# Even attention of a two-layer backbone: values and probabilities split into high and low fp32r parts

## The reference, cut to what matters

```python
att = block_attention(q, concat([k_ctx, k]), concat([v_ctx, v]), scale)   # latent queries
att_ctx = block_attention(q_ctx, k_ctx, v_ctx, scale)                     # context queries

def block_attention(q, k, v, scale):       # swept over blocks of 128 queries
    s = einsum('bqgrd,bkgd->bgrqk', q_blk, k) * scale
    p = softmax(s, axis=-1)
    return einsum('bgrqk,bkgd->bqgrd', p, v)
```

## Time and profile before

| | us |
|---|---|
| median of 3 runs (1912.35 to 1914.12) | 1913.68 |
| the profiled execution's own time | 1911.99 |
| its span | 1910.1 |
| even attention in the trace | 236.6 to 382 |
| TensorE, VectorE, ScalarE, GpSimd busy over the span | 1792.2, 1141.0, 678.4, 178.9 |

### The profile page before, as it was taken

The page is one execution under the profiler, slowest core; times in us unless marked ns, Lnnn a source line. Parts: engine busy times, 40 slices in busy tenths (PEclk is TensorE's granted clock), DMA queues, the critical chain, the costliest instruction groups (busy, mean ns, idle before and its releaser), DMA issues.

```text
span 1910.1 us, 24356 instructions
## 1 busy us (share of the span) xinstructions
PE 1792.2 (94%) x9558; PEld 1503.3 (79%) x9558; DVE 1141.0 (60%) x1750; ACT 678.4 (36%) x1114; POOL 178.9 (9%) x197
## 2 busy tenths in 40 slices
PE   5999889899999999999999999789978899999998
PEld 3677789777888888887777889669966688888776
DVE  3566667667756666644353778877753644434544
ACT  3333156534522222222343431144443442323342
POOL 1168400000300000000000200111100010000000
PEclk9999989999999999999999999899998999999999
DMA  8333100032133345422121121100002222222221
GB/s 327 123 136 111 45 1 1 2 114 85 78 130 133 125 165 187 167 98 81 52 83 50 54 104 67 44 23 1 1 1 98 78 68 108 88 103 94 96 103 66
DMA packets 30996, 166.80 MB, mean 87 GB/s; under 512 B 4144, under 2 KB 4656, under 8 KB 16688
## 3 DMA queue, kind: packets, MB, share of 16 engines
q1 hardware_dynamic: 29024, 163.60, 23.7%
q10 hardware_dynamic: 1872, 1.82, 0.3%
HBM read 163.31 MB, written 2.10 MB: 87 GB/s over the span
## 4 chain that ended last, share of the span: by engine, by line
PE 83%; DVE 6%; issue 4%; ACT 3%; DMA 1%; DVEq 1%; POOL 1%; POOLq 0%; ACTq 0%; SPq 0%
PE PS L302 12%; PE PS L306 12%; PE PS L304 11%; PE PS L603 7%; PE PS L605 7%; PE PS L604 7%; PE PS L1074 5%; PE PS L344 2%; PE PS L345 2%; PE PS L346 2%; PE PS L1062 2%; DVE w_lo L291 1%; PE PS L336 1%; PE PS L337 1%; PE PS L335 1%
## 5 line engine op out<-in xcount | busy, mean ns | idle before, releaser
L302 PE MATMUL PS<-HT,w_hi 128*128 128x512 f32 (+1 forms) x1232 | 376.7, 354 | 11.5 <-DVE HT L517 6.1
L306 PE MATMUL PS<-HT,w_lo 128*128 128x512 f32 (+1 forms) x1232 | 370.0, 349 | 0.0
L304 PE MATMUL PS<-HT,w_hi 128*128 128x512 f32 (+1 forms) x1232 | 369.2, 348 | 0.0
L291 DVE TENSOR_TENSOR w_lo<-w_raw,w_hi 128x2048 fp32r<-128x2048 f32 x103 | 236.7, 2299 | 162.1 <-ACT w_hi L285 156.2
L603 PE MATMUL PS<-w_hi,a_ring 128*128 128x512 f32 x680 | 275.2, 405 | 15.0 <-DVE a_ring L676 8.0
L604 PE MATMUL PS<-w_lo,a_ring 128*128 128x512 f32 x680 | 267.2, 393 | 0.0
L285 ACT ACTIVATE w_hi<-w_raw 128x2048 fp32r<-128x2048 f32 x103 | 196.3, 1906 | 153.9 <-PEq L635 69.6
L302 PEld LDWEIGHTS PS<-HT,w_hi 128*128 128x128 f32 x1232 | 206.1, 189 | 53.7 <-DVE HT L517 6.6
L306 PEld LDWEIGHTS PS<-HT,w_lo 128*128 128x128 f32 x1232 | 205.9, 189 | 30.8
L304 PEld LDWEIGHTS PS<-HT,w_hi 128*128 128x128 f32 x1232 | 205.9, 189 | 30.7
L973 DVE SCALAR_TENSOR_TENSOR yb<-PS,cws,yb 128x511 f32<-128x511 f32 (+1 forms) x132 | 83.2, 658 | 168.9 <-ACTq L939 165.0
(11 more groups left out here) (307 smaller groups left out, 2845.6 us busy)
## 6 DMA issues: line engine op xcount, KB each, us to landing
w_raw<-wpack SPq DMA_DIRECT2D x103, 1024.0 KB, 4.8
m_raw<-modu SPq DMA_DIRECT2D x80, 512.0 KB, 4.0
mod_raw<-modw SPq DMA_DIRECT2D x8, 1024.0 KB, 11.7
X<-x SPq DMA_DIRECT2D x1, 2048.0 KB, 9.0
out<-X SPq DMA_DIRECT2D x4, 512.0 KB, 2.6
X<-ctx SPq DMA_DIRECT2D x1, 1024.0 KB, 11.3
alnb<-aln ACTq DMA_DIRECT2D x1, 512.0 KB, 4.2
csn<-rope_ev ACTq DMA_DIRECT2D x1, 256.0 KB, 2.5
```

The costliest lines, as they stand in the source:

```text
L291: nc.vector.tensor_tensor(w_lo[r][:, :], w_raw[r][:, :], w_hi[r][:, :].bitcast(F32), ALU.subtract).then_inc(wl_ready, 1)
L302: nc.tensor.matmul(o, wh, xh, start=start, stop=False)
L304: nc.tensor.matmul(o, wh, xl, start=False, stop=False)
L306: last = nc.tensor.matmul(o, wl, xh, start=False, stop=stop)
```

## The change

The even attention gets four functions of its own; the odd attention keeps the old ones.

- Values are kept as `Vh` (rounded by ScalarE) and `Vl` (the difference, by VectorE, once). The transposed probabilities are copied from PSUM to `PTh` by ScalarE as before, rounded now, and VectorE takes the difference of PSUM and `PTh` to `PTl`.
- The value product is three fp32r products per key tile: `Vh` by `PTh`, `Vl` by `PTh`, `Vh` by `PTl`. For the latent units it is made once for two units (256 columns), after the transposes of the next even unit; for the context units once per unit (128 columns).
- TensorE's transposes of u wait until the low part of u-1 has been taken from banks 4 and 5.
- VectorE takes only the reciprocal, into `rinv`; GpSimd multiplies the probabilities by it.
- VectorE copies the output once for two latent units, and in context unit u it copies that of u-1, at the end of the iteration.
- `mod_products` waits for both slots of a pair on one semaphore.

```diff
+        rinv = const("rinv", [P, 2])
...
-        Vev = at("Vev", R_HT + 6 * KIB, [P, NT, 256])
-        PTe = [at(f"PTe{i}", R_HT + (12 + 3 * i) * KIB, [P, TOK]) for i in range(2)]
+        Vh = at("Vh", R_HT + 6 * KIB, [P, NT, 256], F32R)
+        Vl = at("Vl", R_A + 60 * KIB, [P, NT, 256], F32R)
+        PTh = [at(f"PTh{i}", off, [P, NT, 2, P], F32R) for i, off in enumerate((R_HT + 12 * KIB, R_HT + 40 * KIB))]
+        PTl = [at(f"PTl{i}", off, [P, NT, 2, P], F32R) for i, off in enumerate((R_MOD, R_GM))]
...
-        mod_landed = [sem(f"mod_landed{i}") for i in range(KD)]
+        mod_landed = [sem(f"mod_landed{i}") for i in range(4)]
...
+            pe.wait_ge(mod_landed[c], 32)
             for i in range(2):
-                pe.wait_ge(mod_landed[2 * c + i], 16)
...
+        PAIRED = HEADS * LT
+        def products_done(u):
+            return u // 2 + 1 if u < PAIRED else PAIRED // 2 + u - PAIRED + 1
+        def turned_into(u):
+            return (u // 2 % 2, u % 2) if u < PAIRED else (u % 2, 0)
+        def even_pe(pe):
+            U = units(False)
...
+            def scores(u):
+                h, t, nk, k0 = U[u]
+                pe.wait_ge(S("eva", "qTl"), u + 1)
+                if u >= 2:
+                    pe.wait_ge(S("eva", "exp"), u - 1)
...
+                last.then_inc(S("eva", "s"), 1)
+            def values(u, w):
+                h, t, nk, k0 = U[u]
+                b, i = turned_into(u)
+                pe.wait_ge(S("eva", "pTl"), u + w)
+                if products_done(u) > 1:
+                    pe.wait_ge(S("eva", "ocopy"), products_done(u) - 1)
+                else:
+                    pe.wait_ge(S("eva", "vl"), 1)
+                o = PS[:, 7, 0:w * P]
+                for j in range(nk):
+                    vh, vl = (v[:, k0 + j, h // 4 * P:h // 4 * P + P] for v in (Vh, Vl))
+                    ph, pl = (p[:, j, i:i + w, :] for p in (PTh[b], PTl[b]))
+                    nc.tensor.matmul(o, vh, ph, start=j == 0, stop=False)
+                    nc.tensor.matmul(o, vl, ph, start=False, stop=False)
+                    last = nc.tensor.matmul(o, vh, pl, start=False, stop=j == nk - 1)
+                last.then_inc(S("eva", "o"), 1)
+            for u in range(2):
+                q_transpose(u)
+                scores(u)
+            q_transpose(2)
+            for u, (h, t, nk, k0) in enumerate(U):
+                pe.wait_ge(S("eva", "p"), u + 1)
+                if u >= 1:
+                    pe.wait_ge(S("eva", "pTl"), u)
+                for j in range(nk):
+                    last = nc.tensor.transpose(ps2(4, TOK)[:, j * P:(j + 1) * P], Pe[u % 3][:, j * P:(j + 1) * P], ident[:, :])
+                last.then_inc(S("eva", "ptr"), 1)
+                if u % 2 == 0 and 2 <= u <= PAIRED:
+                    values(u - 2, 2)
+                if u > PAIRED:
+                    values(u - 1, 1)
+                if u + 2 < len(U):
+                    scores(u + 2)
+                if u + 3 < len(U):
+                    q_transpose(u + 3)
+            values(len(U) - 1, 1)
+        def even_act(act, scale):
+            U = units(False)
...
+            def exps(u):
+                n = U[u][2] * P
+                if u >= 3:
+                    act.wait_ge(S("eva", "ptr"), u - 2)
+                act.wait_ge(S("eva", "max"), u + 1)
+                nc.scalar.activation(Pe[u % 3][:, 0:n], ps2(2 * (u % 2), n), ACT.Exp, bias=rmax[:, u % 2:u % 2 + 1],
+                                     scale=scale, accum_out=rsum[:, u % 2:u % 2 + 1]).then_inc(S("eva", "exp"), 1)
+            for u in range(3):
+                q_copy(u)
+            exps(0)
+            for u, (h, t, nk, k0) in enumerate(U):
+                if u + 1 < len(U):
+                    exps(u + 1)
+                act.wait_ge(S("eva", "ptr"), u + 1)
+                b, i = turned_into(u)
+                if u >= 4:
+                    reader = u // 2 * 2 - 4 if u < PAIRED else (PAIRED - 4 + 2 * (u - PAIRED) if u < PAIRED + 2 else u - 2)
+                    act.wait_ge(S("eva", "o"), products_done(reader))
+                nc.scalar.activation(PTh[b][:, 0:nk, i, :], ps2(4, nk * P).rearrange("p (j q) -> p j q", q=P), ACT.Copy)\
+                    .then_inc(S("eva", "pT"), 1)
+                if u + 3 < len(U):
+                    q_copy(u + 3)
+        def even_dve(dve, scale):
+            U = units(False)
+            def maxima(u):
+                dve.wait_ge(S("eva", "s"), u + 1)
+                if u >= 2:
+                    dve.wait_ge(S("eva", "exp"), u - 1)
+                m = rmax[:, u % 2:u % 2 + 1]
+                nc.vector.reduce_max(m, ps2(2 * (u % 2), U[u][2] * P), AX_X)
+                dve.drain()
+                nc.vector.tensor_scalar(m, m, -scale, None, ALU.mult).then_inc(S("eva", "max"), 1)
+            def inverse(u):
+                dve.wait_ge(S("eva", "exp"), u + 1)
+                if u >= 2:
+                    dve.wait_ge(S("eva", "p"), u - 1)
+                nc.vector.reciprocal(rinv[:, u % 2:u % 2 + 1], rsum[:, u % 2:u % 2 + 1]).then_inc(S("eva", "inv"), 1)
...
+            def copy_out(u, w):
+                h, t, nk, k0 = U[u]
+                dve.wait_ge(S("eva", "o"), products_done(u))
+                nc.vector.tensor_copy(cat_ev[:, 4 + h, t * P:(t + w) * P], PS[:, 7, 0:w * P]).then_inc(S("eva", "ocopy"), 1)
+            q_low(0)
+            maxima(0)
+            q_low(1)
+            maxima(1)
+            q_low(2)
+            inverse(0)
+            nc.vector.tensor_tensor(Vl[:, :, :], V32[:, :, :], Vh[:, :, :].bitcast(F32), ALU.subtract)\
+                .then_inc(S("eva", "vl"), 1)
+            for u, (h, t, nk, k0) in enumerate(U):
+                if u + 1 < len(U):
+                    inverse(u + 1)
+                b, i = turned_into(u)
+                dve.wait_ge(S("eva", "pT"), u + 1)
+                nc.vector.tensor_tensor(PTl[b][:, 0:nk, i, :], ps2(4, nk * P).rearrange("p (j q) -> p j q", q=P),
+                                        PTh[b][:, 0:nk, i, :].bitcast(F32), ALU.subtract).then_inc(S("eva", "pTl"), 1)
+                if u + 2 < len(U):
+                    maxima(u + 2)
+                q_low(u + 3)
+                if u % 2 == 0 and 2 <= u <= PAIRED:
+                    copy_out(u - 2, 2)
+                if u > PAIRED:
+                    copy_out(u - 1, 1)
+            copy_out(len(U) - 1, 1)
+        def even_pool(pool):
+            for u, (h, t, nk, k0) in enumerate(units(False)):
+                pool.wait_ge(S("eva", "inv"), u + 1)
+                pr = Pe[u % 3][:, 0:nk * P]
+                nc.gpsimd.tensor_scalar(pr, pr, rinv[:, u % 2:u % 2 + 1], None, ALU.mult).then_inc(S("eva", "p"), 1)
...
-                sp.dma_start(mod_raw[i % 4][:, :, :].rearrange("p k c -> p (k c)"), modw[i]).then_inc(mod_landed[i], 16)
+                sp.dma_start(mod_raw[i % 4][:, :, :].rearrange("p k c -> p (k c)"), modw[i]).then_inc(mod_landed[i // 2], 16)
...
-            sp.wait_ge(S("eva", "o"), len(units(False)))
+            sp.wait_ge(S("eva", "o"), products_done(len(units(False)) - 1))
...
-            nc.scalar.activation(Vev[:, :, :], V32[:, :, :], ACT.Copy)
+            nc.scalar.activation(Vh[:, :, :], V32[:, :, :], ACT.Copy)
...
-            attn_pe(pe, "eva", False, units(False))
+            even_pe(pe)
...
-            attn_act(act, "eva", False, units(False), P ** -0.5)
+            even_act(act, P ** -0.5)
...
-            attn_dve(dve, "eva", False, units(False), P ** -0.5, cat_ev, lambda u: None)
+            even_dve(dve, P ** -0.5)
...
+            even_pool(pool)
```

More of the change, by code:

```diff
@@ L1166, in attn_pool, with q_transpose @@
                     q_low(u + 2)
+        PAIRED = HEADS * LT
[5 more added lines that the diff above has]
+            U = units(False)
+            def q_transpose(u):
+                h, t, nk, k0 = U[u]
+                if u >= 1:
+                    pe.wait_ge(S("eva", "qTl"), u)
+                nc.tensor.transpose(PS[:, 6, 0:P], Zq[:, t, h * P:(h + 1) * P], ident[:, :]).then_inc(S("eva", "qtr"), 1)
+            def scores(u):
[3 more added lines that the diff above has]
+                    pe.wait_ge(S("eva", "exp"), u - 1)
+                for a, e in (((0, 512), (512, 768)) if nk == NT else ((0, 256),)):
+                    ks = slice(k0 * P + a, k0 * P + e)
+                    o = PS[:, 2 * (u % 2) + a // 512, 0:e - a]
+                    qh, ql = qTh[u % 2][:, :], qTl[u % 2][:, :]
+                    nc.tensor.matmul(o, qh, KTh[:, h // 4, ks], start=True, stop=False)
+                    nc.tensor.matmul(o, qh, KTl[:, h // 4, ks], start=False, stop=False)
+                    last = nc.tensor.matmul(o, ql, KTh[:, h // 4, ks], start=False, stop=True)
+                last.then_inc(S("eva", "s"), 1)
[21 more added lines that the diff above has]
+                pe.wait_ge(S("eva", "p"), u + 1)
+                if u >= 1:
+                    pe.wait_ge(S("eva", "pTl"), u)
```

(24 more changed lines are left out.)

## The result

| | us |
|---|---|
| kernel before, median of 4 runs (1912.35 to 1915.77) | 1913.90 |
| changed kernel, median of 4 runs (1994.63 to 1999.93) | 1997.41 |
| ratio, 95% interval | 1.0436, 1.0417 to 1.0454 |
| profiled execution of the changed kernel: span | 1996.1 |

The change costs 83.5 us. The forecast was 37.8 us, 1951.5, and its range ended at 1962. The direction was right, the size was not.

A forecast was written before the change was run, and what follows sets the result against it. It took TensorE and a VectorE-ScalarE loop as matched bounds at 3.20 us per latent unit. Terms 27.0 + 9.1 + 1.7 = +37.8 us gave 1951.5 against 1913.68, own range 1943 to 1960, widened to 1938 to 1962.

The forecast's parts named there:

- latent units, low part and pairing: Even attention's latent units: mean 4.10 us instead of 3.20, over 30 units +27.0 us.
- context units, output bank: Context units: loop through the single output bank takes 2.42 us against 1.85, 16 x 0.57 = +9.1 us.
- modulation wait: Kernel start: both pairs of passes wait until 18.05, moving the whole start by +1.7 us, bounds 0 and 1.9.
- GpSimd's multiplication: Even attention: taken at 0.80 us from a copy's row, off the loop and hidden; +7 us at 1.83.
- What bounds the kernel before: Latent units: TensorE and the loop maximum, exp, normalise, next maximum both need the whole 3.20 us.
- The value product and the low part: Latent units: paired product 2.16 us per two units; copy and low part 1.76 us in the loop, replacing normalisation's 0.86.
- both paths: Latent units: 3.97 us by the VectorE and ScalarE loop, 4.23 in every second unit by TensorE's longer path.
- The cover: Latent units: reciprocal, hand-overs and a GpSimd multiplication up to about 1.4 us fit under the wait for `PTl`.
- The rival with GpSimd as the bound: Even attention: GpSimd's multiplication sets the pace; 1958.5 us if it takes 1.83, 1969 if 2.5; chance 0.10.
- `Vl`, which the forecast called hidden: Start of the stage: about 1.8 us on VectorE, hidden while the first unit comes up, 1.8 at most if not.
- The clock: Latent units: rival that TensorE's clock falls to 1.2 GHz in the new gaps, 2014 us; chance 0.04.
- gaps of 1 to 1.4 us: Latent units: TensorE some 70% busy with such gaps; an earlier 1.4 us gap had kept the clock at 1.00.

The follow-up runs named there:

- Experiment 1: Changed kernel without the multiplication by the reciprocal, transposes released by VectorE's reciprocal: 1962.83 us, ratio 1.0262.
- 3, filler: Changed kernel, GpSimd's multiplication kept, with unneeded matmuls while TensorE waits in even latent units and context units: 1963.60 us, ratio 1.0267.
- Experiment 5: Changed kernel without the multiplication, plus 4 unneeded matmuls in each context unit: 1951.84 us, ratio 1.0212.
- experiment 4: Kernel before with only the modulation's semaphores changed, one wait for two slots: 1912.38 us, ratio 1.0001.
- Experiment 8: Kernel before with GpSimd multiplying the even attention's probabilities by VectorE's reciprocal, values still fp32: 1920.16 us, ratio 1.0045.
- 2: Changed kernel with the multiplication back on VectorE behind the reciprocal, GpSimd idle in the stage: 1967.02 us, ratio 1.0277.
- Experiment 9: Kernel before with GpSimd multiplying the probabilities of the 16 context units alone: 1910.97 us, ratio 0.9983.

## Why the prediction was right or wrong

The traces give the stage in two parts: the latent units from the first maximum to the first one of a context unit, and the context units from there to the last output copy.

| us | before | changed | 1, no multiplication | 3, filler | 5, no multiplication, filler |
|---|---|---|---|---|---|
| latent units | 107.95 | 169.34 | 134.48 | 147.85 | 137.32 |
| context units | 33.57 | 57.18 | 54.04 | 45.05 | 44.27 |

Experiment 1's latent part holds one pair with a fall of the clock (1.46 us), which is taken off below. Each term is the difference of two traces that differ by it, so that they add up to the stage's 85.0 us is no evidence of its own.

| term | forecast | measured |
|---|---|---|
| latent units, low part and pairing | +27.0 | 1 against before: +25.1 (by the period of 8.20 a pair, 30 x 0.90 = +27.0) |
| context units, output bank | +9.1 | 5 against before: +10.7 (2.50 us a unit at full clock) |
| modulation wait | +1.7 | ratio 1.0001 (4), interval -2.5 to +2.9 |
| GpSimd's multiplication | 0 | 3 against 1 and 5: 14.8 + 0.8 = +15.6 (by the period, (8.94 - 8.20) / 2, 30 x 0.37 = +11) |
| lower clock, latent units | 0 | changed against 3: +21.5 (10.27 - 8.94 a pair) |
| lower clock, context units | 0 | changed against 3: +12.1 (3.49 - 2.50 a unit, but not in the first ones) |
| sum | +37.8 | +85.0 in the stage; the medians say +83.5 |

**What bounds the kernel before:** nothing speaks against it, but no run tests it alone. The changed kernel takes 0.25 us of TensorE's work away while the loop over maximum, exp and the rest grows. Experiment 8 shortens that loop on VectorE, but puts GpSimd's 2.2 us into the path of the transposes.

**The value product and the low part:** right to a tenth of a microsecond per unit, in both paths (4.31 and 3.88 for 4.23 and 3.97). That the sum of the two comes out at 8.19 for 8.20 is partly luck, since one is over and the other under. Experiment 5, which holds these terms and no others of size, took 1951.84 us where the forecast gave 1951.5; 4 us of clock falls are in it, so this agreement is partly luck too.

**GpSimd's multiplication:** this step failed. It was priced from the row of a copy ("0.80: the multiplication reads one tensor"), bounded above by an operation with two tensors, 1.83. It took 2.25 on the mean. The cover was priced right, "up to about 1.4 us fit": of 2.21 us 0.8 stand out beyond it, and half of that per unit is close to the 0.37 measured. The rival with GpSimd as the bound named the path, and gave 1958.5 to 1969 for 1.83 to 2.5 us; at full clock it took 1963.6. The start of the stage adds to it: the first two maxima of even units are 14.06 us apart, and 10.31 in experiment 1. In the changed kernel the first two multiplications took 5.73 us together (from 245.39) while VectorE took `Vl` (245.12 to 246.86); in experiment 8, which has no `Vl`, they took 4.39. So `Vl`, which the forecast called hidden, very likely cost about 1.3 us by way of GpSimd.

**The clock:** this step failed too, and it is the larger: priced at nothing in the sum and given 0.04 as a rival, it took 33.6 us, more than the other errors together. The forecast took gaps of 1 to 1.4 us for granted and found in the earlier trace rows that 1.4 us had kept the clock. With GpSimd's 2.2 us the gap became 1.96 us, and the clock fell in each pair; without it the gap was 1.22 to 1.25 us in nearly every pair, and the clock fell behind it once in experiment 1 (260.85) and three times in experiment 5 (288.70, 323.00, 373.89). So the gap that the forecast relied on was no safe one either. In the latent units two rivals held apart in the forecast were one chain: the longer wait makes the lower clock. The context units are another matter, since their clock falls without GpSimd's part as well: in experiment 1 after some units at full clock, in experiments 1 and 2 it then stayed at 0.50 with 0.59 us of idle time before each product, and with the filler it stayed at 1.00. The forecast had their period nearly right and no warning of the clock. The earlier trace rows showed context units at 1.00 with TensorE busy 12.85 of 14 us; that was no evidence for units of 2.4 us. What in these units' gaps makes it fall when it does stays open.

**The start:** the delay was right, its price is open: experiment 4's interval holds both the forecast's +1.7 and nothing. The 16 transposes behind the wait took 1.97 us where they had taken 3.42, but the later wait doesn't explain that. Experiment 9 has the old wait with the pause between the slots, and its transposes take 1.97 us too; experiment 5 has the new wait, and they take 3.37 (first the former, then the latter):

```profile
18.08 1.72 PE L389 MATMUL PS<-mod_raw,s 128*32 128x512 f32 x8 [0.49 <-DMA mod_raw<-modw]
...
21.35 1.97 PE L1541 MATMUL PS<-ident,xn 128*128 128x128 f32 x16 [1.54 <-DVE xn L1802]
```

```profile
22.82 3.37 PE L1694 MATMUL PS<-ident,xn 128*128 128x128 f32 x16 [1.52 <-DVE xn L1955]
```

The record of the granted clock gives 1.00 for 21.5 to 25 us in the kernels before and after and in both of these. So the cause of the 1.45 us stays open.

## What to carry to other kernels

Before moving an operation to another engine to relieve the first, find where the first waits: an operation in a waiting time is nearly free where it is (some 4 us on VectorE against 35 on GpSimd). In stages where in-order engines hand one buffer round, write the loop down by the queues' order, and price TensorE's work in it at both clock levels once its share of the period falls. Taking a price from periods alone leaves out the first units of a stage; compare whole stretches. A price that no row of the same form gives needs a range reaching beyond the similar rows, and the rivals that follow from its upper end belong together.

## What the runs showed of the hardware

- GpSimd's multiplication of 128x768 fp32 in place by a per-partition scalar takes 2.21 us, 128x256 takes 0.93. Its difference of two tensors of 768 takes 1.83 and its copy of 1024 takes 1.04; the same multiplication of 768 takes VectorE 0.62. The Trainium skill (GPSIMD Engine Reference, section When to use GPSIMD) calls operations with one input roughly line-rate; for this one the measurement says otherwise, and it decides.
- GpSimd's first two multiplications took 5.73 us together while VectorE took a difference of two tensors in SBUF (1.74 us), and 4.39 us in experiment 8 without it.
- TensorE's granted clock fell from 2.4 to 1.2 GHz behind gaps of 1.96 us once in each 10.27 us of which TensorE was busy 73%: products 0.22 us apart at 310.56 and 0.12 at 312.12. The Trainium skill (TensorE: Matmul & The Clock Gate, section HAM oscillation) describes a loop in which the clock falls in the gap of each round and returns with its work; the trace agrees, though the gaps of that loop are longer waits, for DMA. Behind gaps of 1.22 to 1.25 us it fell once in the latent units of experiment 1 and three times in those of experiment 5. Filling the gaps with discarded matmuls took 34 us off the kernel.
- The lower level can hold itself up, the upper one needed work for it: the same context units ran at 1.00 for some units and then at 0.50 to the end in experiment 1, and at 1.00 with 4 more matmuls each in experiment 5.
- An fp32r product of 128 columns starts 0.11 us after its neighbour at the upper clock level (404.03 and 404.14 in experiment 5), as 160 columns do, and 0.22 us at the lower (446.54 and 446.76 in the changed kernel).
